# Pages' stage: rope key copies and the norm product on GpSimd, the score copy on ScalarE, the maximum held in SBUF

## The chip, the core and the metric

One core of a Trainium2 chip runs the whole kernel in one launch. The core has five engines that work from queues of their own and meet through semaphores: TensorE (PE; its weight loads are listed as PEld), VectorE (DVE), ScalarE (ACT), GpSimd (POOL) and SyncE (SP, which here only issues DMAs). The metric is the device time of one launch in microseconds; lower is better.

## What is computed

One inference step of a two-layer decoder in fp32: 512 prompt tokens and 8 sequences with 8 new tokens each. Layer 0 is latent attention, layer 1 a gated recurrence; each is followed by a convolutional feed-forward block. The change lies in the attention of the 8 sequences over their paged cache:

```python
def attend_seq(args):                      # one of 8 sequences; past = 16 pages x 128 keys
    pt, qn, qr, cn, krn = args
    c_all = concatenate([cache_ckv[layer, pt].reshape(past, KV_LORA), cn])       # 2056 x 256
    kr_all = concatenate([cache_krope[layer, pt].reshape(past, QK_ROPE), krn])   # 2056 x 32
    k_nope = rmsnorm(einsum('lc,chd->lhd', c_all, w_uk), g_kn)                   # 16 heads x 64
    s = einsum('qhd,lhd->hql', qn, k_nope) + einsum('qhr,lr->hql', qr, kr_all)
    p = softmax(where(mask, s * SOFTMAX_SCALE, -inf), axis=-1)
    ctx = einsum('hql,lc->qhc', p, c_all)
    return einsum('qhc,chd->qhd', ctx, w_uv)
```

## The kernel before

The engines' programs are written out by hand; no scheduler sets the order. Each engine runs the functions of its own name (`seq_pe`, `seq_act`, `seq_dve`) in the order of the code, and a `wait_ge` holds everything behind it on that engine. The pages' stage is eight sequences `b` of 16 pages `i`, 128 pages in all, one program step per page on PE, ACT and DVE. Sequence 0 stands alone, sequences 1 to 6 are a loop of three turns (`Fori(0, 3)`, two sequences a turn) on ACT and DVE, sequence 7 stands alone. PE's and SP's parts are `seq_pe` and `page_load`.

One page, 128 keys: PE turns it (`turn`, L1135: two 128x128 transposes of the latent rows into a PSUM bank; each fourth page a third one, L1137, that turns the rope keys of four pages at once). ACT rounds the result into `ct_hi` (`hi_act`, L1224) and DVE writes the rest into `ct_lo` (`lo_dve`, L1299): products are made in split precision, from a high and a low part. `krT` is the stationary operand of the rope product, 96 rows by 128 keys, two buffers: ACT copies the page's 32 rows of `ct_hi` into it twice (L1229, L1230), DVE the 32 rows of `ct_lo` once (L1302). PE makes the page's 18 products of 384 columns (`page_products`, L1168 to L1170) into PSUM banks 0 to 2: 1024 columns of keys by head and 128 columns of unnormalised scores. Then it makes the rope product (L1178), the last matmul of a page, into bank 5 or 6. ACT squares the 1024 key columns (L1281, three pieces). DVE copies the 128 score columns out of bank 2 (L1365, into `a_sb`) and sums the squares by head (L1366, into `ssq`).

Four pages are a group `g`. One page after the group ACT makes one over the norms from its sums (L1236, L1238: Ln, then Exp). DVE, two pages after the group, at `i` = 1, 5, 9 and 13 and before it turns to the next page's `ct_lo`, runs `group_dve`: the scores times one over the norm (L1310), plus the rope product from PSUM (L1315), then the running maximum over two halves (L1320, or L1324 twice).

The tail of a sequence runs among the pages of the next one (`tail_pe`, `tail_dve`, `part_exp`): the maximum is finished (`i` = 2), turned (`i` = 3, L1186), reduced and laid on a diagonal (`i` = 4), and spread over all partitions by a matmul into PSUM bank 7, columns 128 to 255 (`i` = 5, L1189). DVE subtracts it from the scores in four parts (`i` = 6 to 9, L1342), reading that bank; ACT takes the exponentials (L1290, at `i` = 7 to 10); PE multiplies the weights with the pages into bank 7 (`i` = 10 to 13, L1197), after a wait at `i` = 10 until the fourth subtraction has read the bank (`x_sub`). Behind the last sequence the tail runs with nothing beside it. GpSimd has nothing to do in this stage; before and after it, it makes the low parts of weight tiles (`split_lo`, L176).

## Time and profile before

| | us |
|---|---|
| median of three runs | 2076.72 |
| lowest and highest run | 2071.84, 2079.54 |
| the profiled execution | 2064.28 |
| its span, first to last instruction | 2062.5 |
| the pages' stage in it | about 308 to 862 |

| engine, whole span | busy us | share |
|---|---|---|
| PE | 1958.5 | 95% |
| PEld | 1869.7 | 91% |
| DVE | 1150.1 | 56% |
| ACT | 828.6 | 40% |
| POOL | 505.3 | 24% |

Times are read from the profiled execution, in us from the start of its span. A PE matmul is recorded with an end that is modelled and overlaps the next one, so a page's time is better read from the start of one rope product (L1178) to the next than from busy shares. A row of the timeline has start, duration, engine, line, operation, output and inputs, and in brackets how long the engine had been idle and what released it. The share of the DMA engines in the stage is 0.13 and PE waits for no page there.

### The profile page before, as it was taken

How to read it: one execution, taken by the hardware profiler on the slowest of the kernel's cores; microseconds unless marked ns; L12 is line 12 of the kernel's file. 1: busy time of each engine (PE TensorE's matmuls, PEld its weight loads, DVE VectorE, ACT ScalarE, POOL GpSimd, SP SyncE). 2: the span in 40 equal slices, each digit the busy share in tenths (PEclk: the TensorE clock that was granted, in tenths of full speed). 3: DMA queues.
4: the chain of work that ended last, by engine and by line, in shares of the span. 5: the costliest groups of instructions: out<-in, count | busy, mean ns of one | idle time of the engine just before them, and what ended most of it. 6: DMA issues, size and time to landing. Idle time of an engine off the chain costs nothing.

```text
span 2062.5 us, 37092 instructions
## 1 busy us (share of the span) xinstructions
PE 1958.5 (95%) x13333; PEld 1869.7 (91%) x13333; DVE 1150.1 (56%) x2191; ACT 828.6 (40%) x1645; POOL 505.3 (24%) x222
## 2 busy tenths in 40 slices
PE   7979999999999999799999999999879999999998
PEld 7867659999999999699999999999879999999997
DVE  3676756766676667438715515527663881552642
ACT  4444556656665666332212212145664221221220
POOL 2230000000000000154333333353225433333431
PEclk9998999999999999999999999999989999999999
DMA  5321001111111110032222222232213222322232
GB/s 141 62 62 34 24 1 42 30 45 35 35 29 44 35 35 24 29 90 72 82 82 82 82 82 82 82 103 65 59 41 100 77 77 84 90 82 82 86 88 75
DMA packets 251864, 131.49 MB, mean 64 GB/s; under 512 B 43009, under 2 KB 249538, under 8 KB 251666
## 3 DMA queue, kind: packets, MB, share of 16 engines
q1 hardware_dynamic: 251666, 129.68, 22.6%
q8 instruction: 77, 1.26, 0.3%
q14 instruction: 45, 0.37, 0.1%
q10 hardware_dynamic: 76, 0.18, 0.0%
HBM read 126.21 MB, written 3.61 MB: 63 GB/s over the span
## 4 chain that ended last, share of the span: by engine, by line
PE 77%; DVE 14%; ACT 5%; issue 3%; DMA 1%; DVEq 0%; ACTq 0%; POOL 0%
PE ps L182 16%; PE ps L183 16%; PE ps L185 16%; PE ps L1168 6%; PE ps L1170 5%; PE ps L1169 5%; PE ps L1197 3%; PE ps L980 2%; PE ps L955 2%; DVE ssq L1366 1%; PE ps L211 1%; DVE arena L1679 1%; DVE arena L1934 1%; PE ps L1135 1%; DVE split L1682 1%
## 5 line engine op out<-in xcount | busy, mean ns | idle before, releaser
L182 PE MATMUL ps<-split,whi 128*128 128x288 f32 x3024 | 856.6, 298 | 30.5 <-DVE arena L1900 13.1
L183 PE MATMUL ps<-split,whi 128*128 128x288 f32 x3024 | 852.6, 297 | 0.0
L176 POOL TENSOR_TENSOR wlo<-raw,whi 128x1024 fp32r<-128x1024 f32 x191 | 461.2, 2415 | 1462.0 <-ACT whi L171 1461.9
L185 PE MATMUL ps<-split,wlo 128*128 128x288 f32 x3024 | 647.4, 296 | 0.0
L182 PEld LDWEIGHTS ps<-split,whi 128*128 128x128 f32 x3024 | 573.1, 190 | 34.5 <-issue 29.9
L183 PEld LDWEIGHTS ps<-split,whi 128*128 128x128 f32 x3024 | 574.3, 190 | 0.7
L185 PEld LDWEIGHTS ps<-split,wlo 128*128 128x128 f32 x3024 | 489.4, 189 | 0.0
L171 ACT CAST whi<-raw 128x1024 fp32r<-128x1024 f32 x191 | 199.0, 1042 | 381.7 <-DMA raw<-in_ffn_w_up 225.6
L1168 PE MATMUL ps<-split,split 128*128 128x384 f32 x768 | 268.5, 350 | 10.0 <-DVE split L1299 8.2
L1170 PE MATMUL ps<-split,split 128*128 128x384 f32 x768 | 257.8, 336 | 0.0
L1169 PE MATMUL ps<-split,split 128*128 128x384 f32 x768 | 257.2, 335 | 0.0
L1281 ACT ACTIVATE arena<-ps 128x384 f32<-128x384 f32 (+1 forms) x384 | 171.8, 456 | 118.8 <-PE ps L1170 114.7
L284 DVE TENSOR_TENSOR xT<-xT,ps 128x576 f32<-128x576 f32 (+1 forms) x64 | 48.3, 754 | 289.5 <-PE ps L185 289.5
L1168 PEld LDWEIGHTS ps<-split,split 128*128 128x128 f32 x768 | 144.3, 188 | 16.1 <-DVE split L1299 12.9
L1366 DVE TENSOR_REDUCE ssq<-arena 128x16 f32<-128x1024 f32 x128 | 155.8, 1217 | 3.0
L1599 ACT ACTIVATE arena<-arena 128x592 f32<-128x592 f32 x48 | 33.6, 700 | 280.0 <-DVE arena L1667 280.0
L1169 PEld LDWEIGHTS ps<-split,split 128*128 128x128 f32 x768 | 144.6, 188 | 0.0
L1170 PEld LDWEIGHTS ps<-split,split 128*128 128x128 f32 x768 | 144.1, 188 | 0.0
L1365 DVE COPY arena<-ps 128x128 f32<-128x128 f32 x128 | 37.3, 292 | 132.2 <-ACT arena L1281 131.3
L1679 DVE TENSOR_TENSOR arena<-arena,work 128x576 f32<-128x576 f32 x48 | 92.3, 1924 | 1.6
L1224 ACT CAST split<-ps 128x256 fp32r<-128x256 f32 (+1 forms) x128 | 50.8, 397 | 67.3 <-PE ps L1135 37.7
L1197 PE MATMUL ps<-arena 128*128 128x257 f32 x256 | 64.6, 399 | 13.0 <-DVE arena L1342 10.3
(249 smaller groups left out, 2015.6 us busy)
## 6 DMA issues: line engine op xcount, KB each, us to landing
raw<-in_ffn_w_up SPq DMA_DIRECT2D x96, 512.0 KB, 3.8
raw<-in_ffn_w_down SPq DMA_DIRECT2D x48, 512.0 KB, 3.9
arena<-in_cache_ckv SPq DMA_DIRECT2D x128, 128.0 KB, 2.0
raw<-in_rec_w_in SPq DMA_DIRECT2D x16, 512.0 KB, 3.9
raw<-in_attn_w_o SPq DMA_DIRECT2D x8, 512.0 KB, 4.1
raw<-in_rec_w_out SPq DMA_DIRECT2D x8, 512.0 KB, 4.2
raw<-in_attn_w_down SPq DMA_DIRECT2D x7, 512.0 KB, 7.9
raw<-in_attn_w_uq SPq DMA_DIRECT2D x48, 64.0 KB, 2.2
```

Of the source, the lines that this page charges most:

```text
L171: act.copy(whi[:, t % RING, :], raw[:, t % RING, :]).then_inc(w_hi, 1)
L176: pool.tensor_tensor(wlo[:, t % RING, :], raw[:, t % RING, :], f32(whi[:, t % RING, :]), ALU.subtract).then_inc(w_lo, 1)
L182: pe.matmul(o, wh, a, start=first, stop=False)
L183: pe.matmul(o, wh, b, start=False, stop=False)
L185: mm = pe.matmul(o, wl, a, start=False, stop=last)
L1168: pe.matmul(ps[:, j, 0:384], ct(ct_hi, i)[:, k, :], uk[:, 0, k, col], start=(k == 0), stop=False)
L1169: pe.matmul(ps[:, j, 0:384], ct(ct_hi, i)[:, k, :], uk[:, 1, k, col], start=False, stop=False)
L1170: mm = pe.matmul(ps[:, j, 0:384], ct(ct_lo, i)[:, k, :], uk[:, 0, k, col], start=False, stop=(k == 1))
L1197: mm = pe.matmul(ps[:, 7, 0:KL + 1], s_all[par][0:n, k, :], rhs, start=(k == 0), stop=(k == SEQ_BLOCKS - 1))
L1281: act.activation(dst, src, ACT.Square).then_inc(kb_sq, 1)
L1366: dve.tensor_reduce(ssq[:, (i // 4) % 2, (i % 4) * NH:(i % 4 + 1) * NH], sqk[:, i % 2, :].rearrange("p (h e) -> p h e", e=DN), AX.X, ALU.add)\
L1679: ch(dve.tensor_tensor(hf[:, j, :], hf[:, j, :], rs[0], ALU.mult))
```

## The change

Four steps of the pages' stage go elsewhere; the arithmetic stays the same.

- The three copies into `krT` go from ACT (two) and DVE (one) to GpSimd (`rope_pool`), under one semaphore `kr_in` instead of `kr_hi` and `kr_lo`. They wait until the rope product two pages back is done.
- The copy of the score columns goes from DVE to ACT, behind the page's third square.
- The product with one over the norm goes from DVE to GpSimd (`group_pool`); DVE's `group_dve` waits for it (`g_s1`).
- The spread maximum is copied by ACT from PSUM into SBUF (`mb`, `max_kept`, at `i` = 6), the subtractions read it there, and PE at `i` = 10 waits for that copy (`x_mbs`) and no longer for the fourth subtraction.

GpSimd's program for the stage is `sample_pool`, written out for all 128 pages. Two output semaphores at the kernel's end are replaced by older ones that are free by then; nothing is issued or waited for in another order there.

```diff
-            pe.wait_ge(kr_hi, b * PAGES + i + 1)
-            pe.wait_ge(kr_lo, b * PAGES + i + 1)
+            pe.wait_ge(kr_in, b * PAGES + i + 1)
...
                 if i == 10:
-                    pe.wait_ge(x_sub, 4 * b + 4)
+                    pe.wait_ge(x_mbs, b + 1)
...
             act.copy(ct_all(ct_hi, i), ps[:, 3 + i % 2, 0:n]).then_inc(t_hi, 1)
-            if i >= 2 or not first(b):
-                act.wait_ge(b_mm, b * PAGES + i - 1)
-            if i % 4 == 0:
-                act.wait_ge(t_hi, b * PAGES + i + 1)
-            act.copy(krT[0:DR, i % 2, :], rope_rows(ct_hi, i))
-            act.copy(krT[DR:2 * DR, i % 2, :], rope_rows(ct_hi, i)).then_inc(kr_hi, 1)
...
             for i in range(PAGES):
+                if tail and i == 6:
+                    max_kept(act, b - 1)
...
                     act.activation(dst, src, ACT.Square).then_inc(kb_sq, 1)
+                g, q0 = i // 4, 0 if par else 256
+                if i % 4 == 0 and (i >= 8 or not first(b)):
+                    act.wait_ge(g_s1, b * 4 + g - 1)
+                act.copy(a_sb[g % 2][:, i % 4, :], ps[:, 2, q0:q0 + HQ]).then_inc(a_ev, 1)
...
+        def max_kept(act, b):
+            act.wait_ge(x_mb, b + 1)
+            if not first(b):
+                act.wait_ge(x_sub, 4 * b)
+            act.copy(mb, ps[:, 7, P:2 * P]).then_inc(x_mbs, 1)
...
+        def rope_pool(pool, b, i):
+
+            n = b * PAGES + i
+            pool.wait_ge(t_lo, n - i % 4 + 1)
+            if n >= 2:
+                pool.wait_ge(b_mm, n - 1)
+            if n:
+                pool.wait_ge(kr_in, n)
+            if n % 4 == 3 and n > 4:
+                pool.wait_ge(g_s1, n // 4)
+            pool.tensor_copy(krT[0:DR, i % 2, :], rope_rows(ct_hi, i))
+            pool.tensor_copy(krT[DR:2 * DR, i % 2, :], rope_rows(ct_hi, i))
+            pool.tensor_copy(krT[2 * DR:3 * DR, i % 2, :], rope_rows(ct_lo, i)).then_inc(kr_in, 1)
+
+        def group_pool(pool, b, g):
+
+            n = b * 4 + g
+            pool.wait_ge(kr_in, min(4 * n + 7, PAGES * NB))
+            pool.wait_ge(g_rs, n + 1)
+            pool.wait_ge(a_ev, 4 * n + 4)
+            if b >= 2:
+                pool.wait_ge(x_ctx, b - 1)
+            dst = s_all[b % 2][:, 4 * g:4 * g + 4, :].rearrange("p a (h t) -> p (a h) t", t=TS)
+            pool.tensor_tensor(dst, a_sb[g % 2].rearrange("p a (h t) -> p (a h) t", t=TS),
+                               ssq[:, g % 2, :].unsqueeze(2).to_broadcast([P, 4 * NH, TS]), ALU.mult).then_inc(g_s1, 1)
+
+        def sample_pool(pool):
+            rope_pool(pool, 0, 0)
+            for n in range(PAGES * NB):
+                if n + 1 < PAGES * NB:
+                    rope_pool(pool, (n + 1) // PAGES, (n + 1) % PAGES)
+                if n % 4 == 1 and n > 1:
+                    group_pool(pool, (n // 4 - 1) // 4, (n // 4 - 1) % 4)
+            group_pool(pool, LAST, 3)
...
-                v = part(s_all[par], i - 6)
-                dve.tensor_tensor(v, v, ps[:, 7, P:2 * P].unsqueeze(1).to_broadcast([P, len(PARTS[i - 6]), HQ]),
+                dve.tensor_tensor(v, v, mb.unsqueeze(1).to_broadcast([P, len(PARTS[i - 6]), HQ]),
```

In `lo_dve`, `group_dve` and `seq_dve` the third `krT` copy, the product and the score copy with their waits are taken out.

DVE, sequence 7, pages 5 and 6: page 5's score copy and sums, `group_dve` for group 0, the next page's `ct_lo`, page 6 and the first subtraction. Before:

```order
L1365 COPY arena<-ps 128x128 [waits kb_sq]
L1366 TENSOR_REDUCE ssq<-arena 128x16
L1310 TENSOR_TENSOR arena<-arena,ssq 128x512 [waits a_ev,g_rs]
L1315 TENSOR_TENSOR arena<-arena,ps 128x512 [waits b_mm,g_s1]
L1320 TENSOR_TENSOR arena<-arena 128x256 [waits x_max,g_s]
L1299 TENSOR_TENSOR split_640_61<-ps,split_640_60 128x256 [waits b_mm,t_hi]
L1302 CAST krT<-split_640_61 32x128
L1365 COPY arena<-ps 128x128 [waits kb_sq]
L1366 TENSOR_REDUCE ssq<-arena 128x16
L1342 TENSOR_TENSOR arena<-arena,ps 128x640 [waits x_mb]
```

DVE at the same place in the changed kernel (its lines L1397, L1348, L1353, L1305 and L1375 are L1366, L1315, L1320, L1299 and L1342 of before):

```order
L1397 TENSOR_REDUCE ssq<-arena 128x16 [waits kb_sq]
L1348 TENSOR_TENSOR arena<-arena,ps 128x512 [waits b_mm,g_s1]
L1353 TENSOR_TENSOR arena<-arena 128x256 [waits x_max,g_s]
L1305 TENSOR_TENSOR split_640_61<-ps,split_640_60 128x256 [waits b_mm,t_hi]
L1397 TENSOR_REDUCE ssq<-arena 128x16 [waits kb_sq]
L1375 TENSOR_TENSOR arena<-arena 128x640 [waits x_mbs]
```

Ten instructions have become six: the two score copies, the product and the `krT` copy are gone, and the subtraction has two operands in SBUF instead of one.

GpSimd in the changed kernel, one group of four pages in a later sequence, from one product (L1330) to the next (before, its queue is empty here):

```order
L1330 TENSOR_TENSOR arena<-arena,ssq 128x512 [waits a_ev,x_ctx,g_rs,kr_in]
L1317 CAST krT<-split_640_60 32x128 [waits kr_in,g_s1,b_mm,t_lo]
L1318 CAST krT<-split_640_60 32x128
L1319 CAST krT<-split_640_61 32x128
L1317 CAST krT<-split_640_60 32x128 [waits kr_in,b_mm,t_lo]
L1318 CAST krT<-split_640_60 32x128
L1319 CAST krT<-split_640_61 32x128
```

The copies of page `i` + 1 stand ahead of the product at `i` = 1, 5, 9 and 13, so the product starts only when they are done; two more such triples follow before the next product.

ACT, sequence 7, pages 5 and 6. Before:

```order
L1281 ACTIVATE arena<-ps 128x256 [waits kb_mm]
L1224 CAST split_640_60<-ps 128x256 [waits kb_mm,t_ps]
L1229 CAST krT<-split_640_60 32x128 [waits b_mm]
L1230 CAST krT<-split_640_60 32x128
L1281 ACTIVATE arena<-ps 128x384 [waits sq_ok,kb_mm]
```

ACT at the same place in the changed kernel:

```order
L1277 ACTIVATE arena<-ps 128x256 [waits kb_mm]
L1281 COPY arena<-ps 128x128
L1291 COPY arena<-ps 128x128 [waits x_sub,x_mb]
L1224 CAST split_640_60<-ps 128x256 [waits kb_mm,t_ps]
L1277 ACTIVATE arena<-ps 128x384 [waits sq_ok,kb_mm]
```

Each page's two `krT` copies have left ACT and one score copy has come; once in a sequence the copy of the maximum (L1291) stands between two pages.

## Rows read from the trace of the kernel before

**Rows 1.** Window 315:842: length, busy us (instructions) PE, PEld, DVE, ACT, POOL; clock, DMA.

```profile
315.00:842.00 527.00, 505.70 (x2969) 486.85 (x2967) 364.98 (x727) 330.88 (x871) 0.00 (x0) 1.00 0.13 35
```

**Rows 2.** Timeline of PE, sequence 3: rope products ending pages 1, 2, 3, 8 to 11.

```profile
511.25 0.23 PE L1178 MATMUL ps<-qr_s,krT 96*128 96x128 f32 x1
...
514.66 0.23 PE L1178 MATMUL ps<-qr_s,krT 96*128 96x128 f32 x1
...
519.37 0.23 PE L1178 MATMUL ps<-qr_s,krT 96*128 96x128 f32 x1
...
537.30 0.23 PE L1178 MATMUL ps<-qr_s,krT 96*128 96x128 f32 x1
...
540.95 0.23 PE L1178 MATMUL ps<-qr_s,krT 96*128 96x128 f32 x1
...
544.39 0.22 PE L1178 MATMUL ps<-qr_s,krT 96*128 96x128 f32 x1
...
551.83 0.23 PE L1178 MATMUL ps<-qr_s,krT 96*128 96x128 f32 x1
```

**Rows 3.** Waits of PE's loads and matmuls, 315 to 842: total us, times, longest.

```profile
PEld ps L1168 <- DVE split L1299: 12.9, 17, 1.2
...
PE ps L1197 <- DVE arena L1342: 10.3, 7, 1.5
...
PE ps L1168 <- ACT arena L1281: 0.8, 2, 0.5
```

**Rows 4.** Timeline of DVE, sequence 3, page 1 with the group's work.

```profile
511.87 0.29 DVE L1365 COPY arena<-ps 128x128 f32<-128x128 f32 x1 [1.15 <-ACT arena L1281]
512.19 1.22 DVE L1366 TENSOR_REDUCE ssq<-arena 128x16 f32<-128x1024 f32 x1
513.33 0.68 DVE L1310 TENSOR_TENSOR arena<-arena,ssq 128x512 f32<-128x512 f32 x1
514.04 0.69 DVE L1315 TENSOR_TENSOR arena<-arena,ps 128x512 f32<-128x512 f32 x1
...
515.66 0.42 DVE L1299 TENSOR_TENSOR split<-ps,split 128x256 fp32r<-128x256 f32 x1
```

**Rows 5.** Timeline of PE, sequence 3: the first context products, behind page 10.

```profile
546.10 2.43 PE L1197 MATMUL ps<-arena 128*128 128x257 f32 x10 [1.49 <-DVE arena L1342]
```

**Rows 6.** Timeline of ACT, sequence 3: the group's Exp, behind page 4.

```profile
523.79 0.26 ACT L1238 ACTIVATE ssq<-ssq 128x64 f32<-128x64 f32 x1
```

**Rows 7.** Groups by line, 315 to 842, ACT: busy us, mean ns, idle before.

```profile
L1230 ACT CAST krT<-split 32x128 fp32r<-32x128 f32 x126 | 37.5, 298 | 1.5
```

**Rows 8.** Timeline of POOL at other places, by size of instruction.

```profile
0.22 0.10 POOL L2181 MEMSET const-float32-0.0<- 128x1 f32 x1 [0.22 <-issue]
...
120.53 1.25 POOL L608 TENSOR_TENSOR split<-raw,split 128x256 fp32r<-128x256 f32 x1
...
907.72 1.56 POOL L261 TENSOR_TENSOR work<-work 128x576 f32<-128x576 f32 x1 [2.41 <-ACT work L248]
909.23 2.39 POOL L176 TENSOR_TENSOR wlo<-raw,whi 128x1024 fp32r<-128x1024 f32 x1
```

**Rows 9.** Timeline of POOL and DVE in the first feed-forward block.

```profile
1011.99 2.40 POOL L176 TENSOR_TENSOR wlo<-raw,whi 128x1024 fp32r<-128x1024 f32 x1 [5.90 <-ACT whi L171]
...
1023.20 2.39 POOL L176 TENSOR_TENSOR wlo<-raw,whi 128x1024 fp32r<-128x1024 f32 x1 [4.37 <-ACT whi L171]
...
1012.03 2.98 DVE L1679 TENSOR_TENSOR arena<-arena,work 128x576 f32<-128x576 f32 x1
...
1024.93 1.28 DVE L1679 TENSOR_TENSOR arena<-arena,work 128x576 f32<-128x576 f32 x1
```

**Rows 10.** Timeline of DVE, ACT and PE in the last tail, behind sequence 7.

```profile
847.92 2.62 DVE L1342 TENSOR_TENSOR arena<-arena,ps 128x640 f32<-128x640 f32 x4 [0.89 <-PE ps L1189]
...
848.77 2.42 ACT L1290 ACTIVATE arena<-arena 128x640 f32<-128x640 f32 x4 [5.93 <-DVE arena L1342]
...
850.59 9.66 PE L1197 MATMUL ps<-arena 128*128 128x257 f32 x32 [2.71 <-ACT arena L1290]
```

More of the change, by code:

```diff
@@ L1092, in build @@
         run = area(A_V + 512, 2 * P)
+        mb = area(A_V + 768, P)
         x_run = sem("x_run")
@@ L1099, in build @@
         pg_in = [sem(f"pg_in{i}") for i in range(8)]
-        kr_hi, kr_lo = sem("kr_hi"), sem("kr_lo")
+        kr_in, x_mbs = sem("kr_in"), sem("x_mbs")
         t_ps, t_hi, t_lo, kb_mm, kb_sq, a_ev, b_mm, sq_ok = (
@@ L1222, in hi_act @@
             if i % 4 == 0 and (i or not first(b)):
-                act.wait_ge(kr_hi, b * PAGES + i)
+                act.wait_ge(kr_in, b * PAGES + i)
             act.copy(ct_all(ct_hi, i), ps[:, 3 + i % 2, 0:n]).then_inc(t_hi, 1)
-            if i >= 2 or not first(b):
-                act.wait_ge(b_mm, b * PAGES + i - 1)
-            if i % 4 == 0:
-                act.wait_ge(t_hi, b * PAGES + i + 1)
-            act.copy(krT[0:DR, i % 2, :], rope_rows(ct_hi, i))
-            act.copy(krT[DR:2 * DR, i % 2, :], rope_rows(ct_hi, i)).then_inc(kr_hi, 1)
         def group_act(act, b, g):
@@ L1297, in lo_dve @@
             if i % 4 == 0 and (i or not first(b)):
-                dve.wait_ge(kr_lo, b * PAGES + i)
+                dve.wait_ge(kr_in, b * PAGES + i)
             dve.tensor_tensor(ct_all(ct_lo, i), ps[:, 3 + i % 2, 0:n], f32(ct_all(ct_hi, i)), ALU.subtract).then_inc(t_lo, 1)
-            if i % 4 == 0:
-                dve.wait_ge(t_lo, b * PAGES + i + 1)
-            dve.tensor_copy(krT[2 * DR:3 * DR, i % 2, :], rope_rows(ct_lo, i)).then_inc(kr_lo, 1)
+        def rope_pool(pool, b, i):
[10 more added lines that the diff above has]
+            pool.tensor_copy(krT[2 * DR:3 * DR, i % 2, :], rope_rows(ct_lo, i)).then_inc(kr_in, 1)
@@ L1362, in seq_dve @@
                 n = b * PAGES + i
-                q0 = 0 if par else 256
                 dve.wait_ge(kb_sq, 3 * n + 3)
-                dve.tensor_copy(a_sb[(i // 4) % 2][:, i % 4, :], ps[:, 2, q0:q0 + HQ]).then_inc(a_ev, 1)
                 dve.tensor_reduce(ssq[:, (i // 4) % 2, (i % 4) * NH:(i % 4 + 1) * NH],
@@ L1416, in sample_act @@
             group_act(act, LAST, 3)
+            max_kept(act, LAST)
             for c in range(4):
@@ L1979, in build @@
         yn = area(R1, 2, D)
-        s_y = [sem("s_y0"), sem("s_y1")]
         def out_pe(pe):
@@ L2000, in out_dve @@
                 if i >= 2:
-                    dve.wait_ge(s_y[i % 2], 16 * (i // 2))
+                    dve.wait_ge(s_x[i % 2], 16 + 16 * (i // 2))
                 dve.tensor_copy(yn[0:n, i % 2, :].rearrange("p (a b) -> p a b", a=2), ps[0:n, b:b + 2, :])\
@@ L2009, in out_store @@
                 dst = O["y_prompt"][0, i * P:(i + 1) * P, :] if i < 4 else O["y_sample"].rearrange("b t d -> (b t) d")
-                sp.dma_start(dst, yn[0:n, i % 2, :]).then_inc(s_y[i % 2], 16)
+                sp.dma_start(dst, yn[0:n, i % 2, :]).then_inc(s_x[i % 2], 16)
         @block.sync
@@ L2055, in _ @@
             sp.wait_ge(S["store"], 96)
-            sp.wait_ge(s_y[0], 48)
-            sp.wait_ge(s_y[1], 32)
+            sp.wait_ge(s_x[0], 64)
+            sp.wait_ge(s_x[1], 48)
         @block.gpsimd
@@ L2066, in _ @@
                 split_lo(pool, t)
+            sample_pool(pool)
             for d in range(LEAD):
```

7 lines of the change are left out of this document (1 added, 6 removed).

## The prediction

> **What bounds the kernel now.** I read the busy shares first, then the stage by windows, PE's page steps, what PE waits for, and last the DVE chain behind those waits. In the middle of the pages' stage PE is busy 505.70 of 527 us at a clock of 1.00 (the 2.4 GHz level), while DVE has 365 and ACT 331 [rows 1]: PE bounds it, and neither helper is full. So the change can only give back what PE stands still. The page steps show where. From the end of page 1 to that of page 2 there are 3.41 us, PE's own work on a page [rows 2]. Page 3 takes 4.71, 0.11 of it the third transpose (half of the two other transposes' 0.22 of PE), so 1.19 are lost; page 9 takes 3.65, so 0.24; page 11 takes 7.44, of which 3.41 are its products, 2.43 the first ten context products and 0.11 a transpose, so 1.49 are lost [rows 2, 5]. The wait table has the same over the stage: 12.9 us in 17 waits of the page's first loads for `ct_lo`, 10.3 in 7 for the fourth subtraction, 0.8 in 2 for the squares behind the loop's turn [rows 3]. That is 24.0 us, with some 2 more of page 9 that no wait names: about 26, 1.3% of the kernel, is all that can be had here.
>
> The 17 waits are seven at page 3, seven at page 7 and three in sequence 0. At page 3 the chain from the end of page 1 is: square, score copy (starts 511.87), sums (512.19), product (starts 513.33, and 0.71 later the addition starts), addition (514.04), two maxima, and `ct_lo` of page 3 at 515.66 [rows 4]. PE ended page 2 with the product of 514.66 [rows 2] and needs that `ct_lo`. This is the wait that ends last.
>
> **The change, part by part, in the order of what it is worth.**
>
> *The subtraction reads SBUF.* PE no longer waits at page 10 for DVE's fourth subtraction but for ACT's copy of the maximum, made four pages earlier, and the first exponential, made three earlier. All of the 10.3 us goes [rows 3]: -10.3. What is late next there: DVE still owes `ct_lo` of page 11, but PE first has 2.43 us of context products [rows 5], longer than the 1.49 it waited and the 0.42 of `ct_lo` [rows 4]. No new wait.
>
> *Score copy and product leave DVE's chain.* The copy took 0.32 (511.87 to 512.19) and the product 0.71 less the overlap of 0.08 between the end of the sums (512.19 + 1.22 = 513.41) and its own start, so 0.63 [rows 4]. The chain is 0.95 shorter. Of 1.19 at the long places (seven page 3s and two of sequence 0 with two maxima each) 0.24 stay; page 7 has one maximum and loses less than 0.95, so nothing stays there, nor at the third place of sequence 0. Left: 9 x 0.24 = 2.2 of 12.9, so -10.7 [rows 3].
>
> *GpSimd's copies.* No row has a GpSimd copy of 32x128. The bounds are 0.10 for a memset of one column and 1.25 for a two-input instruction of twice the columns [rows 8]. The two long rows, 1.56 for 576 and 2.39 for 1024, lie on 0.5 + 1.87 ns a column, which gives 0.74 for 128 columns with two inputs; the 1.25 row lies 0.27 above that line. I take **0.6**, a little under 0.74, for one input. Three make 1.8 us, and they may take until the rope product two pages on, 2 x 3.41 = 6.8 us. Per group there are twelve copies and a product of 0.5 + 512 x 1.87 ns = 1.45: 7.2 + 1.45 = 8.7 of the four pages' 13.75. Hidden; cost 0. The cover is gone at 12c + 1.45 = 13.75, c = 1.02.
>
> *The product on GpSimd.* It needs the group's Exp, which ended at 524.05 [rows 6], about 0.3 later with ACT's score copy in front, and the copies of the page after next, which start with the end of page 4 (about 523.2) and take 1.8: so it starts at about 525.1 and ends at 526.6. DVE would take it after page 5's sums, about 1.6 us behind page 5's end, near 528.1. There are 1.5 us of slack; cost 0. It is gone at 3c = 3.3, c = 1.1.
>
> *ACT.* Two copies of 0.298 leave each page [rows 7], one copy of 128 columns comes; in between from PSUM I take 0.3 by the same row, between nothing and the 0.37 that 256 columns take. ACT gets 0.3 a page lighter. Behind the loop's turn ACT is what PE waits for, and 0.6 us of copies stood in front of the square: -0.8 [rows 3]. At page 9, ACT is behind its queries of page 8 and loses 0.24 in each of six sequences; I give back all: -1.4. The score copy adds 0.3 in front of `ct_hi` at page 3: that is ready two us before DVE asks for it, cost 0. The copy of the maximum holds page 7's `ct_hi` for 0.3 once in a sequence, cost 0 by the same cover.
>
> *The last tail* has no cover. DVE's score copy saves 0.32; GpSimd's product adds 1.45 - 0.69 + 0.1 of hand-over; the copy of the maximum adds 0.33: +0.9. But PE need not wait for all four subtractions (to 850.54): the first ends near 848.7 and its exponential near 849.5, 1.1 us before PE's start at 850.59 [rows 10]. Net -0.2, taken as 0. Launch, the other stages and the renamed semaphores: 0.
>
> *The port between DVE and GpSimd* is the one cost that I put on the other side. A two-input SBUF instruction of DVE that began 0.04 behind GpSimd's 2.40 us one took 2.98, which is 0.62 from GpSimd's end at 1014.39; another that began at 1024.93 took 1.28, which is 0.62 from GpSimd's end at 1025.59 [rows 9]. Both waited GpSimd out and then took 0.62. In the stage the maxima, and now the subtractions too, have two inputs in SBUF, and GpSimd reads SBUF. With c = 0.6 the copies run from 0.2 to 2.0 us behind a page's end and the maxima from 2.4: apart. At page 8 the subtraction is due about 1.6 to 1.9 behind the page's end, just when the copies end and the product of 1.45 starts. If the product gets in first, `ct_lo` of page 10 is some 0.8 late, in seven sequences 5.6; if DVE does, nothing. I take +2, and 0 to 5.6 as bounds.
>
> The rule behind this, from the Trainium skill, "SBUF — State Buffer", section "Who interferes with whom": a VectorE instruction with two SBUF inputs and a GpSimd instruction that reads SBUF exclude each other for a whole instruction, the first to start winning. The trace agrees: the two took 2.98 and 1.28, and both end 0.62 behind GpSimd. By the rule taken strictly, every such meeting costs a whole instruction of GpSimd; without it the sum below would be 2 us lower.
>
> **The sum.** -10.3 - 10.7 - 0.8 - 1.4 + 2 = -21.2, rounded to -21. Against the profiled execution that is 2064.28 to 2043; the three runs have a median of 2076.72, 12.4 above it, which I take as the level of the chip that day: 2076.7 - 21 = **2055**.
>
> **The rivals.**
>
> *A, the port is worse.* If copies take 0.8 us or more each, the triple behind page 1 reaches to 2.6 and more, into the maxima, and a maximum waits out a copy: the 0.95 of the chain is given back at 16 of 17 places, and the subtractions meet copies at pages 7 and 8. What stays is the subtraction's own gain and the loop's: 10.3 + 0.8, and at page 8 the 5.6 is lost: -6 to -11, 2066 to 2071. For it: the same wait in rows 9, and a copy price that I can only bound. Against it: 0.6 leaves 0.4 us between.
>
> *B, GpSimd becomes the bound (slower).* The place is `kr_in` ahead of the rope product. It decides from c = 1.02. At the upper bound, 1.25 by the 128x256 row [rows 8], a group takes 12 x 1.25 + 1.45 = 16.5 us against PE's 13.75 without waits: +2.7 in the two groups of each of seven sequences that have no context products, and in four of sequence 0, 18 x 2.7 = 49, against the 23 gained: +26, about 2103; at c = 1.1, where a group takes 14.65, 18 x 0.9 = 16 and the maxima wait too, it is about even. For it: four GpSimd instructions replace what ACT and DVE do in 0.3 and 0.2. Against it: a column costs GpSimd 1.87 ns with two inputs, and there are 128.
>
> *C, the product is late or DVE finds another wait.* If the product takes 3 us or more (its one-over-norm operand is read eight times over, which no GpSimd row shows), DVE stands at the addition and page 3's loss comes back: only the subtraction's gain stays, -10 or less, 2066 to 2077.
>
> *D, more than forecast.* No collision at page 8 and nothing left at page 3: -26, 2051.
>
> **How the numbers follow.** Forecast and D: 0.67 and 0.08 (c under 0.8). A: 0.10. B: 0.08. C: 0.07. Half a per cent is 10.4 us, about what a measurement of this kernel can tell from no change. Faster by more: the forecast, D and a third of A, 0.78. Within: the rest of A, C and the mild end of B, 0.14. Slower by more: 0.08. The range: low end 2051 (D) less the 5 us by which the lowest run lies under the median, 2045; the high end takes in half of A, 2068. Left out are B, the rest of A, most of C and what the chip's own level adds: 2 in 10.
>
> **What would show it.** Right: page steps at page 3 near 3.8, at page 7 near 3.5, at page 11 near 5.95 instead of 7.44; no wait of L1197 for the subtraction inside the stage; GpSimd copies of 0.5 to 0.7; GpSimd busy 60% of the stage; the stage 20 to 24 us shorter and all else alike. A would show maxima or subtractions of over 0.9 us on DVE; B PE waiting for `krT` at L1178 and steps of 4 us everywhere; C DVE idle before the addition, released by GpSimd. The forecast is wrong if a GpSimd copy costs 0.8 or more.

## The result and the profile after

The changed kernel has a median of 2052.74 us over four runs (2044.03 to 2054.80), the kernel before in the same comparison 2075.36 over four (2071.84 to 2079.54): a ratio of 0.9882, 95% interval 0.9855 to 0.9909. That is 22.6 us less. The forecast was 21 less, 2055 us. Timed again with four runs on another chip, the same code gave 2048.39 against 2071.49, 0.9896 (0.9864 to 0.9927), 23.1 less. In the changed kernel the lines have moved: L1317 to L1319 are GpSimd's copies, L1330 its product, L1281 ScalarE's score copy, L1291 its copy of the maximum, L1375 the subtraction, L1305 `ct_lo`, L1348 the addition, L1353 and L1357 the maxima, L1397 the sums, L1169 to L1171 the page's products. L1178 and L1197 are the rope and the context product as before.

Busy time by engine, from the page:

```profile
PE 1963.8 (96%) x13333; PEld 1882.7 (92%) x13333; DVE 1035.9 (51%) x1903; ACT 767.3 (37%) x1525; POOL 652.2 (32%) x638
```

The stage's window, with the columns of [rows 1]:

```profile
315.00:820.00 505.00, 496.56 (x2956) 483.92 (x2955) 286.98 (x445) 269.90 (x752) 141.86 (x407) 1.00 0.14 38
```

VectorE went from 365 to 287 us, ScalarE from 331 to 270, and GpSimd took 142, 28% of the stage. Shares are not where the gain is; the page steps are (from here on a step is the time from the rope product that ends one page to the one that ends the next). PE, sequence 3, rope products that end pages 1, 2, 3, 8, 9, 10 and 11, and the first context products:

```profile
500.80 0.23 PE L1178 MATMUL ps<-qr_s,krT 96*128 96x128 f32 x1
504.21 0.23 PE L1178 MATMUL ps<-qr_s,krT 96*128 96x128 f32 x1
507.87 0.23 PE L1178 MATMUL ps<-qr_s,krT 96*128 96x128 f32 x1
...
525.45 0.23 PE L1178 MATMUL ps<-qr_s,krT 96*128 96x128 f32 x1
528.87 0.23 PE L1178 MATMUL ps<-qr_s,krT 96*128 96x128 f32 x1
532.30 0.23 PE L1178 MATMUL ps<-qr_s,krT 96*128 96x128 f32 x1
532.37 2.38 PE L1197 MATMUL ps<-arena 128*128 128x257 f32 x10
538.04 0.23 PE L1178 MATMUL ps<-qr_s,krT 96*128 96x128 f32 x1
```

Against [rows 2, 5]: page 2 is 3.41 as before, page 3 went from 4.71 to 3.66, page 9 from 3.65 to 3.42, page 11 from 7.44 to 5.74, and L1197 starts 0.07 behind the rope product, with no wait. This table has all places where a step changed, in us, and the stage as the time from the first rope product to the last:

| | before | after | times in the stage |
|---|---|---|---|
| page 3 | 4.71 | 3.66 | 7 |
| page 7 | 3.88 to 3.91 | 3.55 | 7 |
| pages 7, 11, 15 of sequence 0 | 4.17, 4.60, 4.59 | 3.55 each | 1 |
| page 9 | 3.65 | 3.42 | 6 |
| page 11, with context products | 7.45 | 5.74 | 7 |
| page 0 | 3.73 | 3.63 | 6 |
| page 1 behind the loop's turn | 4.11, 4.02 | 5.31, 5.78 | 1 each |
| the stage | 525.56 | 502.24 | |

The subtraction is worth 11.9 us (seven times 1.70), VectorE's chain 12.5 (7.4 at page 3, 2.4 at page 7, 2.7 in sequence 0), page 9 1.4, page 0 0.6, and the loop's turn took 3.0 back: 23.4, and the stage is 23.3 shorter. (Page 3 of sequence 7, 4.63 and 3.56, and page 11 there, 7.34 before, are 0.1 below their rows.)

Waits of the same window (us, times, longest), those of PE and of its sources:

```profile
DVE split L1305 <- ACT split L1224: 27.7, 29, 3.5
...
PE ps L1169 <- DVE split L1305: 3.7, 2, 2.1
DVE split L1305 <- issue: 3.0, 1, 3.0
...
DVE arena L1348 <- POOL arena L1330: 1.4, 1, 1.4
```

The 24.0 us of [rows 3] have become 3.7, in the two places behind the loop's turn. The seven waits of L1197 are gone. VectorE waits for GpSimd's product once, in the last tail.

The chain that was bound, on VectorE in sequence 3 behind page 1, and GpSimd's copies beside it:

```profile
501.42 1.22 DVE L1397 TENSOR_REDUCE ssq<-arena 128x16 f32<-128x1024 f32 x1 [2.45 <-ACT arena L1277]
501.48 0.29 POOL L1318 CAST krT<-split 32x128 fp32r<-32x128 f32 x1
501.81 0.29 POOL L1319 CAST krT<-split 32x128 fp32r<-32x128 f32 x1
502.55 0.68 DVE L1348 TENSOR_TENSOR arena<-arena,ps 128x512 f32<-128x512 f32 x1
503.36 0.89 DVE L1357 TENSOR_TENSOR arena<-arena 128x256 f32<-128x256 f32 x2
504.17 0.42 DVE L1305 TENSOR_TENSOR split<-ps,split 128x256 fp32r<-128x256 f32 x1
```

Beside [rows 4] the sums start at once and the addition follows them. A GpSimd copy of 32x128 lasts 0.29 and the next starts 0.33 later, so three take one microsecond. The product at page 4 of the same sequence:

```profile
512.32 0.26 ACT L1232 ACTIVATE ssq<-ssq 128x64 f32<-128x64 f32 x1
512.40 0.29 POOL L1319 CAST krT<-split 32x128 fp32r<-32x128 f32 x1
512.77 1.08 POOL L1330 TENSOR_TENSOR arena<-arena,ssq 128x512 f32<-128x512 f32 x1
```

It ends at 513.85, and VectorE's addition comes at 516.56, 2.7 us later. The meeting that the prediction feared at page 8, in the same sequence:

```profile
526.82 1.08 POOL L1330 TENSOR_TENSOR arena<-arena,ssq 128x512 f32<-128x512 f32 x1
...
527.20 1.25 DVE L1375 TENSOR_TENSOR arena<-arena 128x512 f32<-128x512 f32 x1
...
528.38 0.41 DVE L1305 TENSOR_TENSOR split<-ps,split 128x256 fp32r<-128x256 f32 x1
```

The subtraction behind page 7 (523.79) took 0.68, this one 1.25: it ends 0.55 behind the product's end at 527.90, as the two rows in [rows 9] ended 0.62 behind GpSimd. It happens once in each of seven sequences, and the page steps 8, 9 and 10 are 3.42, 3.42 and 3.43: PE pays nothing.

### The profile page after: what moved, and what is told of

Read it like the earlier page. It is cut to its first block, busy times and chain, and to the rows that moved or that the text cites. A ratio compares the mean times of both kernels' runs of the same rounds, so it can differ in the third digit from the quotient of the medians.

```text
span 2049.4 us, 37167 instructions
## 1 busy us (share of the span) xinstructions
PE 1963.8 (96%) x13333; PEld 1882.7 (92%) x13333; DVE 1035.9 (51%) x1903; ACT 767.3 (37%) x1525; POOL 652.2 (32%) x638
## 4 chain that ended last, share of the span: by engine, by line
PE 87%; DVE 6%; ACT 4%; issue 2%; DMA 1%; POOL 0%; ACTq 0%; DVEq 0%; POOLq 0%
PE ps L182 18%; PE ps L185 18%; PE ps L183 18%; PE ps L1169 7%; PE ps L1171 6%; PE ps L1170 6%; PE ps L1197 3%; PE ps L955 2%; PE ps L980 2%; PE ps L1136 1%; PE ps L211 1%; DVE arena L1966 1%; PE ps L971 1%; ACT whi L171 1%; DVE work L1941 0%
## 5 line engine op out<-in xcount | busy, mean ns | idle before, releaser
L1169 PE MATMUL ps<-split,split 128*128 128x384 f32 x768 | 268.8, 350 | 4.2 <-DVE split L1305 3.7
L1171 PE MATMUL ps<-split,split 128*128 128x384 f32 x768 | 258.5, 337 | 0.0
L1170 PE MATMUL ps<-split,split 128*128 128x384 f32 x768 | 257.8, 336 | 0.0
L1397 DVE TENSOR_REDUCE ssq<-arena 128x16 f32<-128x1024 f32 x128 | 156.1, 1220 | 186.6 <-ACT arena L1277 186.6
L284 DVE TENSOR_TENSOR xT<-xT,ps 128x576 f32<-128x576 f32 (+1 forms) x64 | 48.3, 754 | 295.9 <-PE ps L185 295.9
L1317 POOL CAST krT<-split 32x128 fp32r<-32x128 f32 x128 | 36.3, 284 | 499.1 <-DVE split L1305 338.3
L1169 PEld LDWEIGHTS ps<-split,split 128*128 128x128 f32 x768 | 144.9, 189 | 5.5 <-DVE split L1305 4.2
L1170 PEld LDWEIGHTS ps<-split,split 128*128 128x128 f32 x768 | 145.1, 189 | 0.0
L1171 PEld LDWEIGHTS ps<-split,split 128*128 128x128 f32 x768 | 144.7, 188 | 0.0
L1556 DVE TENSOR_TENSOR arena<-ps,work 128x288 f32<-128x288 f32 x56 | 25.6, 458 | 114.5 <-PE ps L185 112.7
L1711 DVE TENSOR_TENSOR arena<-arena,work 128x576 f32<-128x576 f32 x48 | 76.2, 1588 | 1.6
L1705 DVE TENSOR_TENSOR arena<-arena,ps 128x288 f32<-128x288 f32 x48 | 21.8, 454 | 108.7 <-PE ps L185 104.4
```

Source lines behind the costliest of these rows:

```text
L1169: pe.matmul(ps[:, j, 0:384], ct(ct_hi, i)[:, k, :], uk[:, 0, k, col], start=(k == 0), stop=False)
L1170: pe.matmul(ps[:, j, 0:384], ct(ct_hi, i)[:, k, :], uk[:, 1, k, col], start=False, stop=False)
L1171: mm = pe.matmul(ps[:, j, 0:384], ct(ct_lo, i)[:, k, :], uk[:, 0, k, col], start=False, stop=(k == 1))
L1397: dve.tensor_reduce(ssq[:, (i // 4) % 2, (i % 4) * NH:(i % 4 + 1) * NH], sqk[:, i % 2, :].rearrange("p (h e) -> p h e", e=DN), AX.X, ALU.add)\
L1711: ch(dve.tensor_tensor(hf[:, j, :], hf[:, j, :], rs[0], ALU.mult))
```

## The experiments

All but the last group give the step table a value in place of an argument. In the tables of this part the time is the median and the kernel before's beside it is from the same chip.

**The maximum alone.** The kernel before, with only the copy of the maximum and PE's new wait (and, as in all kernels below, the two renamed output semaphores):

```diff
+        mb = area(A_V + 768, P)
...
-                    pe.wait_ge(x_sub, 4 * b + 4)
+                    pe.wait_ge(x_mbs, b + 1)
...
-                dve.tensor_tensor(v, v, ps[:, 7, P:2 * P].unsqueeze(1)...
+                dve.tensor_tensor(v, v, mb.unsqueeze(1)...
```

> Only the maximum in SBUF, on the kernel before. Stage is the time from the first rope product to the last (525.56 us before, 502.24 after). My theory (three separate gains: 10.3 from the subtraction, 10.7 from the DVE chain, about 2 from ACT's relief): the step of page 11 falls from 7.44 to 5.95 in seven sequences, page 3 stays at 4.71, the stage is 10.4 us shorter, 515.2; time 0.5% lower. Rival (the chains are one: with the subtraction out of the way the late ct_lo of page 11 takes its place, since DVE still does copy and product there): page 11 at 6.4 or more, the stage at most 7 us shorter. The loop's turn: if the longer steps at page 1 of sequences 3 and 5 (5.31 and 5.78 instead of 4.11 and 4.02) come from GpSimd's program being fetched, they stay near 4.1 here.

Measured: 2058.55 against 2073.83, ratio 0.9935 (0.9911 to 0.9959). The stage is 513.63, 11.9 shorter; page 11 takes 5.74, page 3 4.71 as before, the loop's turn 4.13 and 4.06. The expectation had 10.4 and a page 11 of 5.95; its rival, a late `ct_lo` in the subtraction's place, did not come. So this part is worth the same alone and with the others, and it touches nothing else.

**The rope copies alone.** The kernel before, with only the three copies moved to GpSimd.

```diff
-            act.copy(krT[0:DR, i % 2, :], rope_rows(ct_hi, i))
-            act.copy(krT[DR:2 * DR, i % 2, :], rope_rows(ct_hi, i)).then_inc(kr_hi, 1)
...
+            pool.tensor_copy(krT[0:DR, i % 2, :], rope_rows(ct_hi, i))
+            pool.tensor_copy(krT[DR:2 * DR, i % 2, :], rope_rows(ct_hi, i))
+            pool.tensor_copy(krT[2 * DR:3 * DR, i % 2, :], rope_rows(ct_lo, i)).then_inc(kr_in, 1)
```

> Only the three krT copies on GpSimd; score copy, product and maximum as before. My theory: no gain in the DVE chain, as L1302 lies behind ct_lo; ACT's relief takes page 9 from 3.65 to 3.42 in six sequences: stage 1.5 us shorter but for the loop's turn. Loop's turn: if ACT alone sets it, the two steps fall from 4.1 to 3.5 (1.2 us more gain); if GpSimd's program or a shorter DVE program makes DVE's turn longer, they rise to 5 or more and eat the gain (stage 525 to 527).

Measured: 2049.67 in one run, the stage 519.48, 6.1 shorter: page 3 4.58, page 7 3.76, page 9 3.42, page 11 7.32, the turn 3.47 and 3.58. Page 9's loss was ScalarE's copies: it goes with them. The 0.13 at pages 3, 7 and 11 was not expected: VectorE's sums now start 0.21 behind the score copy's start in place of 0.32, and what holds them back in the kernel before is not shown. GpSimd's long written-out program is there, but for its 32 products, while the turn is cheap, so that program alone is not what made the turn dear.

**The score path alone.** The kernel before, with the score copy on ScalarE and the product on GpSimd.

```diff
+                act.copy(a_sb[g % 2][:, i % 4, :], ps[:, 2, q0:q0 + HQ]).then_inc(a_ev, 1)
...
+            pool.tensor_tensor(dst, a_sb[g % 2].rearrange("p a (h t) -> p (a h) t", t=TS),
+                               ssq[:, g % 2, :].unsqueeze(2).to_broadcast([P, 4 * NH, TS]), ALU.mult).then_inc(g_s1, 1)
```

> Only the score copy on ACT and the product on GpSimd; krT copies on ACT and DVE and the maximum as before. My theory: page 3 falls from 4.71 to about 3.7, page 7 from 3.9 to 3.54, page 11 from 7.44 to about 6.5 (its chain is 0.95 shorter too), in sum 7 x 0.95 + 7 x 0.35 + 7 x 0.95 + 2.5 = 18: stage about 508. Rival (ACT, which keeps its krT copies and gets the score copy, becomes late): page 9 above 3.65 and page 3 above 3.9, stage 512 or more. GpSimd's program is short here (32 products): a loop's turn still above 5 would speak for DVE's own program, one near 4.1 for GpSimd's.

Measured: 2046.57 in one run, the stage 506.73, 18.8 shorter. Page 3 is 3.66 and page 7 3.55, all of the change's own; page 9 is 3.80, worse than before's 3.65, because ScalarE now has the score copy and still its own two; the turn 4.18 and 4.44. Page 11 is 6.42 with the old wait in place. Its wait, over the stage:

```profile
PE ps L1198 <- DVE arena L1379: 3.1, 7, 0.5
```

(L1198 is the context product and L1379 the subtraction there.) Before it was 10.3 in seven [rows 3]. A shorter chain on VectorE brings the fourth subtraction forward, so the same microsecond at page 11 is won once by the chain and once by the copy of the maximum. The three parts alone give 11.9 + 6.1 + 18.8 = 36.8, together 23.3. Page 11 is 8.1 of the 13.5 between: 7 x (1.70 + 0.13 + 1.03) less 7 x 1.70. The turn is 3.5 more: +0.05, -1.1 and +0.5 alone, +3.0 together. The rest is pages 0, 3, 7 and 9 and sequence 0.

**GpSimd slower.** The changed kernel with 3, 6 or 9 spare copies of 32x128 ahead of each page's three; what the kernel computes stays the same.

```diff
+            for k in range(3):          # 3, 6 or 9
+                pool.tensor_copy(spare[0:DR, k, :], rope_rows(ct_hi, i))
             pool.tensor_copy(krT[0:DR, i % 2, :], rope_rows(ct_hi, i))
```

> The changed kernel with three more GpSimd copies a page, into spare columns, ahead of the three into krT (six a page). A copy of 32x128 starts 0.33 us behind the one before it, so a page's copies take 2.0 us, which is what I had assumed for three at 0.6 (1.8). This tests the cover that the prediction named. Theory: nothing is late, page steps stay as they are (3.66 at page 3, 3.54 at 7, 5.74 at 11), the stage stays at 502 to 503. Rival A (port): the copies reach into maxima and subtractions; page 3 at 4 us or more and the stage 507 or more.

> Nine copies a page: 3.0 us, as if each of the three cost 1.0, the prediction's edge between hidden and bound. GpSimd needs 12 x 1.0 + 1.1 = 13.0 of the four pages' 13.8 us. Theory: throughput still suffices, but the copies behind page 1 end 3.2 us behind it and cover DVE's maxima (1.8 to 2.7 behind its end), so page 3 goes to about 4.2 and the stage to 506 to 512. Rival (B alone, no port): steps unchanged, stage under 504.

> Twelve copies a page: 3.9 us, as if each of the three cost 1.3. GpSimd needs 16 x 1.0 + 1.1 = 16.9 us a group against PE's 13.8. Rival B's price was +2.7 in each of 18 groups. Theory: GpSimd is the bound in those 18 groups at about 3.1 each, 56 us: stage about 555 to 560, PE waits for krT at the rope product, time above that of the kernel before. If the stage stays under 525, GpSimd's queue is not what the two buffers make me believe.

The expectations took 0.33 for each spare copy. It was 0.24, from one start to the next. A spare copy keeps fp32 and a real one rounds; no run tells whether that is the reason. GpSimd in the kernel with six spare copies, in sequence 3:

```profile
537.90 1.46 POOL L1319 COPY arena<-split 32x128 f32<-32x128 f32 x6 [2.02 <-DVE split L1306]
539.32 0.28 POOL L1320 CAST krT<-split 32x128 fp32r<-32x128 f32 x1
539.64 0.29 POOL L1321 CAST krT<-split 32x128 fp32r<-32x128 f32 x1
```

So a page's copies take 1.7, 2.4 and 3.2 us, as if a real copy cost 0.57, 0.8 and 1.05.

| copies of a page, us | time | before | stage | page 3 | DVE addition waits for product, last tail included |
|---|---|---|---|---|---|
| 1.0 (the change) | 2052.74 | 2075.36 | 502.24 | 3.66 | 1.4, once |
| 1.7 | 2058.59 | 2075.45 | 504.25 | 3.66 | 1.4, once |
| 2.4 | 2036.20 | 2075.45 | 502.97 | 3.67 to 3.79 | 2.8, 8 times |
| 3.2 | 2079.69 | 2075.45 | 539.07 | 3.9 to 7.4 | 40.7, 23 times |

The times of the three, and of the kernel before beside them, are single runs and carry the scatter told of below; the stage does not. At 0.57 a copy, close to the forecast's own assumption, no page step changes; the stage is 2.0 longer by the loop's turn alone (5.69 and 7.34). At 0.8 the stage loses nothing that counts, though VectorE's maxima meet the copies (444 ns in the mean against 425). The expectation had a page 3 of 4.2 and a stage of 506 or more there, and missed. At 1.05 it breaks: 36.8 longer than the change's, where 53 to 58 were expected, with PE waiting for `krT`. The waits of that kernel inside the stage:

```profile
DVE arena L1351 <- POOL arena L1333: 39.3, 22, 2.6
...
PE ps L1170 <- DVE split L1306: 26.6, 21, 2.0
...
PE ps L1179 <- POOL krT L1322: 0.9, 3, 0.3
```

(L1351 is the addition, L1333 the product, L1170 the page's first product, L1306 `ct_lo`, L1179 the rope product.) PE hardly waits for `krT`. It waits for `ct_lo`, that one for VectorE's addition, and that for GpSimd's product, which starts only when a page's copies are done. GpSimd and PE in that kernel, sequence 2, behind page 1:

```profile
450.84 2.19 POOL L1319 COPY arena<-split 32x128 f32<-32x128 f32 x9 [0.16 <-POOL krT L1322]
...
454.01 1.08 POOL L1333 TENSOR_TENSOR arena<-arena,ssq 128x512 f32<-128x512 f32 x1
...
455.12 0.69 DVE L1351 TENSOR_TENSOR arena<-arena,ps 128x512 f32<-128x512 f32 x1 [2.06 <-POOL arena L1333]
...
456.73 0.42 DVE L1306 TENSOR_TENSOR split<-ps,split 128x256 fp32r<-128x256 f32 x1
...
457.21 0.47 PE L1170 MATMUL ps<-split,split 128*128 128x384 f32 x1 [2.01 <-DVE split L1306]
```

This page's step is 7.37, and the stall explains 2.0 of the 3.7 over 3.66. The rest is the clock, in windows (the last three columns are granted clock, DMA share, GB/s):

```profile
457.00:458.00 1.00, 0.79 (x3) 0.80 (x4) 1.00 (x2) 0.00 (x0) 1.00 (x5) 0.74 0.06 8
458.00:459.00 1.00, 1.00 (x4) 1.00 (x4) 0.77 (x3) 0.00 (x0) 0.88 (x3) 0.50 0.00 0
459.00:461.00 2.00, 2.00 (x8) 2.00 (x8) 0.56 (x1) 0.87 (x2) 0.81 (x4) 0.53 0.00 0
461.00:462.00 1.00, 1.00 (x7) 1.00 (x6) 0.00 (x0) 0.49 (x1) 1.00 (x5) 1.00 0.00 0
```

Behind a stall of 2.0 us the clock stood at 0.50, the 1.2 GHz level, for some three microseconds. Four of the seven page 3s show it (7.29 to 7.37); the others, 3.9 to 5.8, don't, though one of them had a stall of 2.00 too. So a long stall can cost nearly twice its own length.

The row of 1.7 shows the port from the other side. At page 8 of each of its seven sequences the subtraction got in first, and it was the product that took longer, 1.40 in place of 1.08:

```profile
534.18 0.80 DVE L1378 TENSOR_TENSOR arena<-arena 128x512 f32<-128x512 f32 x1
534.52 1.40 POOL L1333 TENSOR_TENSOR arena<-arena,ssq 128x512 f32<-128x512 f32 x1
```

These kernels test how long GpSimd's queue may be, and not one thing that rival A assumed: a single copy of 0.8 us that a maximum would have to wait out. The spare copies are short ones, and a maximum that meets one waits for a short one.

**The loop's turn.** Only here the forecast's sign was wrong. Four kernels are the changed one with no arithmetic changed: unaltered; with 48 or 24 one-column memsets on VectorE ahead of the stage, which move the loop's code in VectorE's program; and with the loop written out.

```diff
+            for k in range(48):         # or 24
+                dve.memset(ssq[:, 0, k:k + 1], 0.0)
             lo_dve(dve, 0, 0, 0)
```

```diff
-            with act.Fori(0, 3) as r:
+            for r in range(3):
...
-            with dve.Fori(0, 3) as r:
+            for r in range(3):
```

> The changed kernel with the loop over sequences 1 to 6 written out on ACT and DVE. Theory: the 1.9 and 2.4 us lost at page 1 of sequences 3 and 5 are the loop's turn (jump and fetch of the loop's code), so both steps fall to 3.43, the stage from 502.24 to 498.0, and the time by 0.2%. Rival (fetching of straight code is as slow, or DMA traffic of fetches stalls an engine anywhere): steps of over 4 us appear at other places and the stage stays at 501 or more.

> The changed kernel with 48 tiny memsets of DVE ahead of the stage, which move the loop's code by 48 instructions in DVE's program and do nothing else. At the loop's turn the trace of the changed kernel shows 5 and 6 packets of instructions, those of the kernel before and of the krT copies alone 2. Theory (where the loop's head lies in DVE's program decides how much is fetched again): the steps at page 1 of sequences 3 and 5 leave 5.31 and 5.78 by over 0.5 us, probably down to 3.5. Rival (a shorter DVE chain runs dry at every turn, wherever the code lies): they stay within 0.3 us.

> The changed kernel, unaltered. If the loop's turn is a property of where the loop's code lies, it repeats: steps of page 1 of sequences 3 and 5 of 5.3 and 5.8 us again (within 0.3), five or six instruction packets of the queue at each, and the stage 502.2 within 0.5. If the turn was an accident of one execution, it is 3.5 to 4.1 this time and the stage 498 to 499. The stretch from the first to the last L284 line of the feed-forward blocks is expected to differ from the 1182.91 of the first profile by several us although no instruction differs (1162 to 1184 so far over the kernels). Time 2052 within 6, ratio to before 0.988.

> The changed kernel with 48 one-column memsets of VectorE ahead of the stage, timed. If placement sets the turn: turns of 3.5 us again, stage 498.2, that is 4.0 shorter than the changed kernel on the same chip, less what the memsets take ahead of the stage: ratio to before 0.986 to 0.988. If the turn of its first profile was an accident: turns anywhere from 3.5 to 6, stage 498 to 503.

> The changed kernel with the loop of sequences 1 to 6 written out on ScalarE and VectorE, timed beside the changed kernel on one chip. No turn at all: page 1 steps 3.44, stage 497.6 against 502.2, so 4.6 us less than the changed kernel, a ratio to before of 0.984 to 0.987 against its 0.988. If the longer program costs something elsewhere, that shows as steps over 3.6 in the stage or a median no lower than the changed kernel's.

> The changed kernel with 24 one-column memsets of VectorE ahead of the stage, half the shift of the other. If placement sets the turn, the value is again fixed by the code and may be anything from 3.5 to 6 us, the number of instruction packets going with it: two packets with a turn near 3.5 to 4.1, five or six with 5 or more. If packets and turn do not go together, fetching is not what the turn waits for. The rest of the stage stays: page 3 3.66, page 11 5.74.

| kernel | time | before | ratio (95%) | stage | steps behind the turns |
|---|---|---|---|---|---|
| the change | 2052.74 | 2075.36 | 0.9882 (0.9855 to 0.9909) | 502.24 | 5.31, 5.78 |
| the change again | 2048.39 | 2071.49 | 0.9896 (0.9864 to 0.9927) | 504.37 | 5.68, 7.36 |
| 48 memsets | 2043.65 | 2075.45 | one run | 498.22 | 3.51, 3.49 |
| 48 memsets, again | 2044.01 | 2071.49 | 0.9872 (0.9854 to 0.9889) | 498.05 | 3.43, 3.43 |
| 24 memsets | 2047.82 | 2071.49 | one run | 498.26 | 3.63, 3.43 |
| loop written out | 2043.41 | 2073.83 | 0.9839 (0.9801 to 0.9877) | 497.56 | none (3.43) |
| loop written out, again | 2042.24 | 2071.49 | 0.9835 (0.9796 to 0.9874) | 497.56 | none (3.43) |

The turn is dear in both executions of the change and in the three kernels with spare copies, whose VectorE program is the same, and cheap in all three executions with the code moved by a few dozen instructions that do nothing. So it is where the loop's code lies, not what it does, and it repeats in kind though not in size: 5.68, 7.36 and a stage of 504.37 were not within the 0.3 and 0.5 expected. What VectorE, ScalarE and PE do there in the change's first profile:

```profile
493.81 0.28 DVE L1385 COPY arena<-ps 128x128 f32 x1
497.08 0.42 DVE L1305 TENSOR_TENSOR split<-ps,split 128x256 fp32r<-128x256 f32 x1 [3.00 <-issue]
...
494.87 0.37 ACT L1224 CAST split<-ps 128x256 fp32r<-128x256 f32 x1 [2.27 <-PE ps L1171]
...
497.56 0.44 PE L1169 MATMUL ps<-split,split 128*128 128x384 f32 x1 [1.62 <-DVE split L1305]
```

VectorE is done at 494.09 and its operand is ready from ScalarE at 495.24, yet it starts 1.84 later, and 3.00 idle stand under "issue": it waits for nothing that the trace shows. At the same turn of the kernel with 48 memsets (second execution) it starts as soon as ScalarE's part is there:

```profile
500.44 0.42 DVE L1305 TENSOR_TENSOR split<-ps,split 128x256 fp32r<-128x256 f32 x1 [1.08 <-ACT split L1224]
```

In both kernels VectorE is done 1.40 us ahead of PE's rope product (494.09 to 495.49, 499.36 to 500.76), and ScalarE starts 0.62 and 0.72 ahead of it. So the memsets hardly shifted the engines against each other; VectorE's start alone differs, 1.59 behind that rope product against 0.32 ahead of it. The queue that brings instructions (named q14 in the DMA part; packets, MB, share) moved this in 16 us around the turn, 484 to 500 in the change and 490 to 506 in the kernel with 48 memsets:

```profile
q14 instruction: 5, 0.04, 0.9%
```

```profile
q14 instruction: 2, 0.02, 0.4%
```

Over both turns the counts are 5 and 6 for the change, 6 and 6 in its second profile, 2 and 2 for 48 memsets, 3 and 2 for 24, 2 and 2 before. The parts alone have 2 or 3 at each turn, the kernels with spare copies, whose turns are 5.4 to 7.3, have 5 to 7. More fetches and a dear turn go together in all these profiles. That the fetch is what VectorE waits for fits all of this, but no row shows which engine a packet is for, so it is argued and not shown; nor do the runs say what about the place decides.

The 7.36 of the second profile has the clock in it as well: PE waited 2.17 us there, and then

```profile
630.00:632.00 2.00, 2.00 (x10) 2.00 (x9) 0.75 (x2) 0.49 (x1) 0.00 (x0) 0.71 0.02 4
632.00:634.00 2.00, 2.00 (x8) 2.00 (x7) 0.00 (x0) 0.49 (x1) 0.00 (x0) 0.50 0.00 0
```

Its matmuls stand in the timeline with 0.53 us in place of 0.33. The first profile had a wait of 2.10 at the same turn and no fall.

**The loop written out, as a version.** With the loop written out the change is at 0.9839 and 0.9835 of the kernel before on two chips; beside it on the second chip the change has 0.9896. The stage is 6.8 us shorter than in the change's profile there and 4.7 shorter than in its first, the medians 6.1 apart. The intervals, 0.9796 to 0.9874 and 0.9864 to 0.9927, overlap, so by time alone it is not shown to be faster than the change. Its stage is shorter place by place: the turns are gone, and page 3 is 3.58 in place of 3.66.

## Why the prediction was right, step by step

*The subtraction*: forecast 10.3, got 11.9. The place and the mechanism held, and the experiment with the maximum alone has the same 11.9. The size was taken from PE's recorded waits and a page 11 of 5.95 instead of 5.74. Ten context products were put at their recorded 2.43 us [rows 5], but a recorded matmul's end overlaps what comes next: without the wait they add 5.74 - 3.41 - 0.11 = 2.22.

*VectorE's chain*: forecast 10.7, got 12.5. What should have stayed at nine long places was 0.24 each; what stayed is 3.66 - 3.52 = 0.14 at page 3, and next to nothing in sequence 0. The chain is 1.04 shorter, not 0.95: the addition starts 1.75 behind page 1's end (502.55 to 500.80), where it started 2.79 behind it. The forecast took 0.08 off for the overlap of sums and product, but the addition overlaps the sums as the product did. Of the steps by name, page 3 near 3.8 was 3.66, page 7 near 3.5 was 3.55.

*GpSimd's copies*: assumed 0.6, were 0.29 (0.33 from start to start). The cover was far larger than counted; the price was off by nearly two. The nearest rows were two-input instructions on 128 partitions; a copy with one input and a quarter of the partitions costs much less than the 0.74 of their line. Which of the two makes the difference, no run tells. GpSimd is 28% busy in the stage, not 60%.

*The product*: assumed 1.45, was 1.08, and its operand read eight times over costs nothing that shows. Its slack was put at 1.5 and was 2.7.

*Where the cover ends*: the forecast said c = 1.02 for GpSimd being the bound and 1.1 for the product being late. At 0.8 nothing was lost, at 1.05 the stage is 36.8 longer, and no run lies between: the number fits, though with the product's real 1.08 the same sum gives 1.06, so that its closeness is partly luck. The place didn't hold: it was to be PE at `kr_in`, and it is VectorE at the product, by the mechanism of rival C. In the rows of sequence 2 the copies start right behind the ones before them (0.16 idle, released by GpSimd itself) and the product behind the copies, so the first who suffers is who waits for the instruction behind the copies.

*The port*: +2 taken, 0 got. The collision at page 8 happens in all seven sequences, as [rows 9] had it (0.57 longer than the subtraction before it, ending 0.55 behind GpSimd's end), but `ct_lo` of page 10, which waits behind it, ended at 528.79 and PE ended page 9 with the rope product of 528.87: it came in time by 0.1. The rule of the Trainium skill, "SBUF — State Buffer", section "Who interferes with whom", is borne out by this: VectorE's instruction began 0.38 behind GpSimd's and ended only 0.55 behind its end, and with three spare copies, where VectorE began first, GpSimd's took 0.32 longer. What the section doesn't tell is whether anyone waits for the one that is held. That it cost nothing here hung on 0.1 us, which the forecast had not worked out. Rival A, which was to come from 0.8 a copy on, did not show at copies that sum up to that: page 3 is at most 3.79. A single copy of 0.8 was not tried.

*ScalarE*: page 9 gave its 1.4, as forecast, and page 0 another 0.6 that was not; either of the last two parts alone gives that 0.6 (3.63), the maximum alone doesn't. The loop's turn was to give 0.8 and took 3.0. The forecast had read the wait there as ScalarE's [rows 3] and asked what its queue would do; with VectorE's loop in another place of its program, VectorE comes after ScalarE there and PE waits for it. This is the step that failed: the turn was asked only of ScalarE, and VectorE's own turn was put at nothing.

*The last tail*: forecast 0 for the step from the last rope product to L1197, got 10.01 against 10.36, -0.35, in both profiles of the change. The maximum alone has 9.74 there. GpSimd's product and the copy of the maximum stand in it as forecast, both shorter than assumed:

```profile
817.39 1.07 POOL L1330 TENSOR_TENSOR arena<-arena,ssq 128x512 f32<-128x512 f32 x1 [10.05 <-ACT ssq L1232]
818.49 0.69 DVE L1348 TENSOR_TENSOR arena<-arena,ps 128x512 f32<-128x512 f32 x1 [1.42 <-POOL arena L1330]
...
822.81 0.27 ACT L1291 COPY arena<-ps 128x128 f32<-128x128 f32 x1 [5.56 <-PE ps L1189]
...
824.85 4.62 PE L1197 MATMUL ps<-arena 128*128 128x257 f32 x10 [2.07 <-ACT arena L1296]
```

This 0.35 did not last. The context products stand at a granted clock of 0.50 until it rises, and the 33rd starts 20.08 behind the last rope product, before 19.94. Behind them the clock fell a second time, which it did not do in the profile before:

```profile
837.51 3.58 PE L1430 MATMUL ps<-arena 128*64 128x64 f32 x64 [0.67 <-DVE arena L1385]
```

```profile
862.76 2.10 PE L1399 MATMUL ps<-arena 128*64 128x64 f32 x64 [0.67 <-DVE arena L1352]
```

The first is the change, at a clock of 0.53, the second the same 64 matmuls before, at 1.00. Together with a third fall (0.57 over 844 to 848) this makes the way from the last rope product to the first L284 36.8 in place of 33.7. The change's second profile has 34.4 and the other kernels 33.2 to 37.1, so it is no cost of the change.

So the terms were -11.9, -12.5, -1.4, -0.6, +3.0, 0 and -0.4 against -10.3, -10.7, -1.4, 0, -0.8, +2 and 0: a sum of -23.8 against -21.2, up to the first context product of the last tail. Four terms were off by 1.6 to 3.8 us and partly cancelled: the two gains came out larger, the port cost nothing, and the turn took the most of that back. That the total is better than its parts is luck.

The spans of the profiled executions don't show this gain: they differ by only 13.1 us, 2062.5 to 2049.4. The stretch from the first to the last L284 line behind the attention has the same code in all kernels and took 1173.7 before, 1182.9 in the change's first profile and 1173.8 in its second; over the fourteen profiles it lies between 1162 and 1185. What makes it scatter is open. In such a kernel a single profile's span can't carry a difference of 20 us; the stage can: away from the loop's turn its steps agree within 0.05 us a page from one execution to the next.

## What to carry to other kernels

Read a bound engine's lost time as steps of a repeated unit, and give each place in that unit its own term: it then shows, too, when two parts of a change win the same microsecond. A helper's price matters only against its cover, so work out the price at which the cover ends, and look for the end not only at the engine that bounds, but at whoever waits for the last instruction in the helper's queue. Where a kernel has a hardware loop near its bound, reckon with its turn changing by microseconds when the loop's code moves, look at that step first when a sum doesn't close, and try the loop written out.
